# Products for an idle TensorE in seven waits of a two-block transformer kernel

## What is computed

```python
def second_block(x, p, ...):
    h = x
    for layer in range(2):
        hn = rmsnorm(h, gains[0])
        mix = mixer_ab(hn, ...) if layer == 0 else mixer_c(hn, ...)
        h = h + rmsnorm(mix, gains[1])
        hn = rmsnorm(h, gains[2])
        ff = jnp.square(jax.nn.relu(hn @ w_up[layer])) @ w_down[layer]
        h = h + rmsnorm(ff, gains[3])
        gate = jax.nn.sigmoid(h @ w_ple_gate[layer])
        h = h + gate * (p[layer] @ w_ple[layer])
    return h
```

## Time and profile before

| | us |
|---|---|
| median of three runs | 3234.21 |
| lowest and highest of them | 3230.03, 3236.12 |
| the profiled execution | 3229.29 |
| its span, first to last instruction | 3227.5 |

### The profile page before, as it was taken

One profiled execution on the slowest core, in us unless ns is written; L12 is line 12 of the kernel. 1 busy time (PEld: TensorE's weight loads), 2 busy tenths in 40 slices (PEclk: granted clock), 3 DMA queues, 4 the chain that ended last, 5 costly groups with the idle time before them and its releaser, 6 DMA issues.

```text
span 3227.5 us, 40309 instructions
## 1 busy us (share of the span) xinstructions
PE 3156.7 (98%) x15026; PEld 2584.5 (80%) x15026; DVE 1127.0 (35%) x2230; ACT 1253.4 (39%) x2260; POOL 1737.8 (54%) x1355
## 2 busy tenths in 40 slices
PE   9999999999999999999999999999999999999999
PEld 7888877787777788788888888877888777788887
DVE  4322322123555533223222664623111249321114
ACT  4323333224444435343323433335333356543334
POOL 5555664555555465456555513236555653565564
PEclk9999999999999999999999999999999999999999
DMA  5333322332222233333333212112333321233332
GB/s 165 100 98 93 91 84 74 91 89 73 68 63 69 66 105 111 85 92 102 95 98 94 79 33 59 37 52 83 101 95 101 92 85 43 72 92 98 98 105 82
DMA packets 149840, 275.58 MB, mean 85 GB/s; under 512 B 16528, under 2 KB 17808, under 8 KB 149520
## 3 DMA queue, kind: packets, MB, share of 16 engines
q1 hardware_dynamic: 149648, 273.02, 28.9%
HBM read 270.86 MB, written 2.10 MB: 85 GB/s over the span
## 4 chain that ended last, share of the span: by engine, by line
PE 92%; DVE 4%; ACT 1%; issue 1%; POOL 1%; DMA 0%; DVEq 0%; SPq 0%; ACTq 0%; POOLq 0%
PE PS L747 90%; PE PS L815 1%; DVE AR L1360 1%; DVE PS L1360 0%; DVE AR L1366 0%; DVE PS L2094 0%; DVE TMP L1360 0%; POOL WL L2521 0%; DVE ACC L1360 0%; ACT TMP L2134 0%; POOL SM L2521 0%; DVE ACC L1366 0%; DVE TMP L1366 0%; ACT HH L2134 0%; DVE HL L1366 0%
## 5 line engine op out<-in xcount | busy, mean ns | idle before, releaser
L2521 POOL TENSOR_TENSOR WL<-RAW,WH 128x512 fp32r<-128x512 f32 x1002 | 1299.6, 1309 | 898.8 <-ACT WH L2134 897.9
L2134 ACT ACTIVATE WH<-RAW 128x512 fp32r<-128x512 f32 x1002 | 619.3, 627 | 1037.5 <-PE PS L747 976.8
L747 PE MATMUL PS<-HH,WH 128*128 128x512 f32 x2264 | 896.7, 396 | 6.6 <-DVE HL L1366 3.2
L747 PE MATMUL PS<-HL,WH 128*128 128x512 f32 x2264 | 884.9, 391 | 3.0 <-DVE HL L1366 2.2
L747 PE MATMUL PS<-HH,WL 128*128 128x512 f32 x2264 | 884.5, 391 | 0.0
L747 PE MATMUL PS<-AH,WH 128*128 128x512 f32 (+1 forms) x1504 | 585.6, 389 | 7.1 <-ACT AH L2134 4.4
L747 PE MATMUL PS<-AL,WH 128*128 128x512 f32 (+1 forms) x1504 | 582.3, 387 | 2.2 <-POOL AL L2521 1.1
L747 PE MATMUL PS<-AH,WL 128*128 128x512 f32 (+1 forms) x1504 | 582.0, 387 | 1.0 <-POOL WL L2521 1.0
L747 PEld LDWEIGHTS PS<-HH,WH 128*128 128x128 f32 x2264 | 427.2, 189 | 99.1 <-issue 11.4
L747 PEld LDWEIGHTS PS<-HL,WH 128*128 128x128 f32 x2264 | 427.1, 189 | 92.7 <-DVE HL L1366 5.0
L747 PEld LDWEIGHTS PS<-HH,WL 128*128 128x128 f32 x2264 | 426.4, 188 | 90.2
(11 more groups left out here) (225 smaller groups left out, 2569.9 us busy)
## 6 DMA issues: line engine op xcount, KB each, us to landing
RAW<-in_wst SPq DMA_DIRECT2D x1002, 256.0 KB, 2.6
X<-in_x SPq DMA_DIRECT2D x8, 256.0 KB, 5.7
TMP<-in_p SPq DMA_DIRECT2D x8, 256.0 KB, 3.1
out<-X SPq DMA_DIRECT2D x8, 256.0 KB, 2.0
AR<-in_dm SPq DMA_DIRECT2D x1, 1024.0 KB, 6.4
AR<-in_mem SPq DMA_DIRECT2D x1, 1024.0 KB, 6.0
CST<-in_cst SPq DMA_DIRECT2D x1, 964.0 KB, 8.2
AR<-in_pos SPq DMA_DIRECT2D x2, 256.0 KB, 3.5
```

The costliest lines, as they stand in the source:

```text
L747: return e.matmul(o, l, r, start=a, stop=z, skip_group_check=True)
L2134: return e.activation(o, a, f, **kw)
L2521: return e.tensor_tensor(o, a, b, op)
```

## The change

A helper `turn_over(o, n)` issues n products of 128x128 by 128x512 into a bank `o` that the step has just taken; both operands are the WH panel in use. Nothing reads the result, and the step's own first product writes over it. It is called in seven places: in `m_fin` 3 and `fin` 3 (4 products each), in `gs` (4), ahead of k = 0 in `u_open` of layer 0 (4) and of layer 1 (6), and in `e_open` of both layers (4 each). In the last four it stands behind all four bank waits and writes to the first of the four banks. In `spread`, for all norms, the bank is now taken before the wait for the factor; before it was taken after it, in `turned`.

```diff
+            def turn_over(o, n):
+
+                p = (len(blocks) - 1) // PT
+                for _ in range(n):
+                    mm(o, WH[:, p % RS, 0:128], WH[:, p % RS, 0:512], True, True)
+
             def spread(n, label, done, col=0):
 
+                o, r = bank(*label), nr(n)
+                if done in (("m_fin", 3), ("fin", 3)):
+                    turn_over(o, 4)
                 e.wait_ge(*at("factor", n))
-                r = nr(n)
-                turned(label, done, lambda t: r[:, t, col:col + 1].to_broadcast([128, 128]), NORM[n][3])
+                for t in range(NORM[n][3]):
+                    z = e.transpose(quarter(o, t), r[:, t, col:col + 1].to_broadcast([128, 128]), ident)
+                z.then_inc(*up("mm", *done))
...
                     o = bank("gs_exp", 2)
+                    turn_over(o, 4)
                     e.wait_ge(*at("g_logs"))
...
                         opened[kind] = [bank("relu", l, m) for m in range(4)]
+                        turn_over(opened[kind][0], (4, 6)[l])
...
                         opened[kind] = [bank(*added(l, m)) for m in range(4)]
+                        turn_over(opened[kind][0], 4)
```

## The result

| | before | after |
|---|---|---|
| median, us (13 runs each, side by side) | 3232.83 | 3224.79 |
| lowest and highest, us | 3228.61, 3236.12 | 3221.40, 3229.55 |
| ratio, with its 95% interval | | 0.9979 [0.9971, 0.9986] |
| the profiled execution, us | 3229.29 | 3225.51 |
| its span, us | 3227.5 | 3223.7 |

The forecast was 3225.3 us. By the ratio the gain is 6.8 us (4.5 to 9.4), where the sum had 7.1; the medians lie 8.0 us apart.

The account below looks back on a forecast made before the run. PE is 98% busy, but fourteen half-clock stretches (52.1 us) hold about 26 us winnable at most. Five stretches or halves, -8.5, and up 1, +1.35, give -7.1 from 3232.4: 3225.3 us; range 3219.5 to 3232.5 (8 in 10).

Parts of the forecast that it names:

- The five stretches: Half-clock stretches or halves at m_fin 3, fin 3, up 0, gate 0, gate 1 should go: 1.7 us each, -8.5 us.
- gs: Four added products fit its 2.19 us wait, bank long free; no half-clock stretch follows: cost 0, gain 0 us.
- Up 1: Layer 1's `u_open`: third bank comes late, six products lie on the path, wait stays empty, stretch stays: +1.35 us.
- Up 0: Layer 0's `u_open`: banks free 0.6 us into the 2.33 us wait, four products fit, cost 0; its stretch goes, -1.7 us.
- Gate 0, gate 1, fin 3, m_fin 3: Four products at each fit inside the wait, so they cost 0 us; at m_fin 3 at worst 0.2.
- The order of bank and factor: Norms in `spread`: bank wait now ahead of the factor's; the later decides in either order, 0 us.
- Given back: Side question whether later waits swallow the gain: waits after up 0 move earlier with PE, so the gain should stay.
- Rival B: Falls move instead of going; half of the five come back elsewhere: -2.9 us, 3229.5 us; chance 0.20.
- Rival C: More goes: two more stretches, at gs and a later one, or up 1 works too: -10.5, 3221.9 us; chance 0.17.
- Rival D: Slower: products are paid, above all at up 1, and the falls stay: 3233.8 to 3235.0 us; chance 0.09.
- Rival E: Banks late everywhere, thirty products on the path, no fall mended: 6.8 us slower, 3239.2 us; chance 0.04.
- The rule weighed: Skill page warns only of idle gaps as long as up 1's; by it filling the other six waits wins nothing.

Follow-up runs that it names:

- e1: Kernel before with the new bank-factor order and thirty added products at up 1 only, behind its four bank waits: 3239.09 us, ratio 1.0029.
- e4: Changed kernel without any added product, only the new order of bank and factor: 3234.47 us, ratio 1.0014 of before.
- e7: Kernel before with no part of the change; the one-column products that sum squares, and alike in `columns`, get 64 columns: 3223.74 us, ratio 0.9974.
- e11: The kernel of e4 run once more, no added products: 3232.33 us, ratio 1.0005 of before.
- e2: Changed kernel with up 1's six products directly behind the first bank wait, the other three bank waits after them: 3222.10 us, ratio 0.9972 of before.
- e5: The kernel of e2 run again, for comparison on the same chip: 3220.22 us, ratio 0.9966 of before.
- e6: The kernel of e5 with the factor's wait again ahead of the bank's in norms without added products: 3221.18 us, ratio 0.9966 of before.
- e8: The edits of e6 and e7 together, plus four products in each of seven more waits: 3214.04 us, ratio 0.9945 of before.
- e9: Changed kernel without the six products at up 1, the other 24 kept: 3223.53 us, ratio 0.9979 of before.
- e10: The changed kernel, unedited, measured again beside e9 and e11: 3225.47 us, ratio 0.9985 of before.

## Why the prediction came out right

- **The total** held: 3225.3 against 3224.79 us. Taking the mean of the four known times as the base (3232.4) and not the profiled execution was right; 13 runs of the kernel before have their median at 3232.83. From the profiled execution the same sum would have given 3222.2. That it is right to half a microsecond is luck: the gain was 6.8 us by the ratio and 4.8 when measured again, the sum lacks the 1.7 us at gs, and the stretches came and went at eight more places that it doesn't have. The mean clock of the profiled execution rose to 0.993 and not to the 0.995 that was said.
- **The five stretches** (-8.5) went as said: four whole ones, and the second half at m_fin 3. The four are no accident of one profile. In the five kernels with no added product at these places (before, e1, e4, e7, e11) a stretch begins at the end of the waits of up 0 and gate 0 or just behind it every time, and at fin 3 and gate 1 every time but in e7; with wide products there is none at the four places in any of seven profiles (after, e2, e5, e6, e8, e9, e10). Thin ones leave it at three of the four and bring no gain. The kernel e4, with no product:

```profile
2158.98:2162.39 3.41, 3.41 (x10) 2.63 (x9) 0.69 (x1) 1.15 (x2) 1.89 (x2) 0.50 0.00 0
2213.59:2217.01 3.42, 3.31 (x7) 2.38 (x8) 2.37 (x4) 2.45 (x5) 1.75 (x2) 0.50 0.00 0
2578.82:2582.23 3.41, 3.41 (x9) 2.63 (x8) 2.36 (x4) 0.51 (x2) 0.90 (x1) 0.50 0.30 77
3182.98:3186.39 3.41, 3.35 (x8) 2.67 (x9) 3.11 (x6) 1.60 (x3) 1.28 (x1) 0.50 0.14 15
```

  The size was a little high: the timeline gives 1.5 to 1.6 us for each, and seven products of 0.225 us, 15 less 8, are 1.58 and not 1.7.
- **gs** was priced wrong for this execution: "0 us" took before's wait of 2.19 us as given. A half-clock stretch ahead of it made TensorE late, the wait was gone, and the four products cost about 1.7 us. The second profile of the change shows the same (four products from 1826.17, gs's own at 1827.88); where no stretch stands ahead (e6, e8, e9) 1.16 or 1.17 us of the wait are left and the price is 0.
- **Up 1** (+1.35) is right in its mechanism. The wait stayed empty, 3.30 us; the products start 0.26 us after the DVE HL row ends; a stretch follows, at 2810.56. From the end of that DVE row to the waited product it was 0.21 us, now 2812.23 - 2809.76 = 2.47. Of the 2.26 more, 0.9 is half-clock time that the six take over from the products behind them, and 1.35 stays. With thirty the mechanism is plain in the timeline as well.
- **Up 0**: the banks were late by 0.78 us where 0.6 was predicted, and 0.38 us of the wait was left. The price, 0, held.
- **Gate 0, gate 1, fin 3, m_fin 3**: 0 us, with 0.28 us or more of idle time left behind the products.
- **The order of bank and factor**: "0 us" was too low by 0.09 us at each norm for which TensorE waits. The argument that the later of two waits decides in either order leaves out that the second wait isn't free when it is the one that ends last. It is about 0.5 us in all; whether falls come on top stays open.
- **Given back**: what the sum had as a side question has a size after all, ahead of waits. The norm of the memory branch shows it, in PE's timelines of the kernel before and of the one with the old order put back:

```profile
1203.35 1.95 PE L747 MATMUL PS<-VC,TMP 128*128 128x1 f32 x16
...
1210.95 0.43 PE L815 MATMUL PS<-CST,SM 128*128 128x128 f32 x2 [1.18 <-DVE SM L1366]
```

```profile
1201.87 1.95 PE L747 MATMUL PS<-VC,TMP 128*128 128x1 f32 x16
...
1209.46 0.69 PE L834 MATMUL PS<-CST,SM 128*128 128x128 f32 x2 [2.68 <-DVE SM L1386]
```

  In the first a half-clock stretch stands right ahead of the wait (1205.91 to 1209.32) and the wait is 1.18 us; in the second there is none ahead of it and the wait is 2.68. The factor doesn't come from TensorE's last products: from the sum of squares to the turned factor it is 7.60 us with the stretch and 7.59 without. So its 1.5 us (sixteen products of 128x256 at 0.213 instead of 0.12 us) were given back whole. In the second kernel a stretch begins inside the wait, at 1208.91, and slows the products behind it. "26 us that could be won at most" is therefore more than there is. The kernel with everything has 6.9 us at half clock instead of 52.1, which is 22.6 us at half speed, and its span fell by 15.8. How much of the other 6.8 was given back in this way isn't shown. The five forecast stretches stand behind their waits, so this didn't touch them.
- **Rival B** (falls that move, 0.20) is partly real, and the sign named for it came: five new places in the profiled execution of after, one of them right where gs's four products run. They aren't chance either: in the second profile of the change they stand at the same five. That is why the profiled pair shows only 3.8 us. But they aren't the work of the products alone: kernels without any have stretches at two of these places as well (1378.65 in e7, 2801.45 in e11). Of the kernel before there is one profile, so how often it has them isn't known, and the ratio of the times and not the pair of profiles has to be read. B and the forecast aren't exclusive, as the chances had them.
- **Rival C** (more goes) didn't come about in this change; what it takes is known now: the bank order at up 1, the wide sums, and seven more waits. **Rival D** is excluded, since the stretches at the four places are gone; but its premise, a fall after microseconds in which PE counts as busy, holds (next point). **Rival E** is excluded by the 4.1 us in front of thirty products.
- **The rule weighed** speaks for products at up 1 alone, the only long wait. The runs decide against it twice: with none there and 24 in the short waits the gain is 0.21%, and in the stretch from 2069 to 2080 us the clock fell with PE counted as busy throughout. The Trainium skill, page "TensorE: Matmul & The Clock Gate", section "Why this matters for your kernels", names only idle gaps as what brings throughput down in the middle of a kernel; here that is too little.

## What to carry to other kernels

Ask for the granted clock in short stretches before anything else when TensorE is "98% busy"; each fall to half cost 1.5 to 1.6 us here, unless a wait right behind it gives them back. Fill the known waits ahead of dense work with wide products, on a bank that has long been free and behind that bank's wait alone: an added product behind four bank waits is behind the latest of them. Don't price such a product by one profile's wait: what comes ahead can eat the wait, as at gs. And look first at products of one column, since widening them cost nothing here and was worth as much as thirty added products.

## What the runs showed of the hardware

- A row of 128x1 products counts as busy and doesn't hold the clock: between 2069 and 2080 us, where such rows stand among 128x128 ones, it fell to 0.50 for 6.82 us with PE busy for 11.00 of 11.00 us, and stayed at 1.00 there with 64 columns. An instruction of 64 columns takes the same time as one of a single column: 2.34 and 2.29 us for twenty, each with its weight load.
- Two waits in front of one instruction: from the last mark to the start it is 0.135 us if the awaited one is the second of them, 0.045 if it is the first, at the same norm.
- The falls repeat in part. In the two profiles of the change the stretches stand at the same places, those at 1820.70 and 2670.62 for instance at 1821.95 and 2671.87. In the two of the kernel with up 1's six behind the first bank (e2, e5) some stand in one and not in the other, at 2198.10 and 2563.33 only in the first. The times of the kernel before spread by 7.5 us; with nearly all falls taken away they spread by 1.2 us.
